# Token transposes moved up beside the inner layer's transposes in a mixture-of-experts loop

## The chip, the cores and the metric

The kernel runs on one core of one Trainium2 chip. The metric is the device time of one execution in microseconds (us), and less is better. TensorE is written PE, its weight loads PEld, VectorE DVE, ScalarE ACT, GpSimd POOL, SyncE SP.

## The reference

A decoder trunk of two layers over 512 tokens of width 1024, in float32. Layer 0 mixes tokens with an RWKV-7 recurrence, layer 1 with dilated window attention, and each layer ends with the mixture that this change is about:

```
h = h + hier_moe(rmsnorm(h, norm_ffn_g[layer]), ...)

# hier_moe: each token takes the best of 4 groups and in it 2 of 4 experts, so 2 of 16
for e in range(N_EXPERTS):                        # 16
    hdn = jax.nn.silu(t @ w_gate[e]) * (t @ w_up[e])   # t: 512 x 1024, hdn: 512 x 512
    y = y + gate[:, e:e + 1] * (hdn @ w_down[e])       # gate is 0 for tokens not routed to e
```

## The kernel before, in words

The function `moe` runs once for each layer. After a router it lists for each expert up to 128 tokens and takes the 16 experts one after another, in rounds: `rounds` unrolls round 0 and round 15 and runs rounds 1 to 14 in a loop of seven passes with two rounds each. All five engines run the same rounds, each with a program of its own, in its own written order; semaphores alone tie them together.

An expert's weights come in six pieces of 1 MB: two halves each of gate, up and down. SP loads a piece into one of six `raw` buffers (`load_piece`, L1442) as soon as DVE has freed one. Each piece is split into a high and a low part, so that a product in full precision is made of three faster ones: ACT writes `whi` (`split_hi`, L1448) and DVE writes `wlo` (`split_lo`, L1452, one piece a round in two halves, L1866). There are four buffers for each part. A `product` on PE is one piece: 12 matmuls of 128x512 (L1459, L1460, L1461).

Around the products, for one expert:

- POOL gathers the expert's token rows into `xg` with an indirect DMA (`fetch`, L1629 and L1632). There is one `xg`, so `fetch` waits until PE has transposed the expert before. Behind it on POOL stands `store_output` of an earlier expert (L1543, L1547), which waits for that expert's output `yo` from ACT, and then for its own DMA.
- `pe_tokens` (L1466 to L1472) transposes `xg` into PSUM banks 0 and 1: 16 transposes of 64x64. It waits for the gather and for DVE to be done with those banks. ACT and DVE then split the result into `xhi` (L1503) and `xlo` (L1508). Both exist twice, so x stands in four tiles, and the tokens of expert e+1 are made while those of e are read.
- `pe_gate` and `pe_up` are two products each, into banks 2 and 3. ACT makes `sg` (L1515), DVE makes `hid` (L1522).
- `pe_hidden` (L1475 to L1481) transposes `hid` into banks 4 and 7: 8 transposes of 64x64. ACT and DVE split it into `hhi` (L1527) and `hlo` (L1532).
- `pe_down` is two products, into banks 5 and 6, and ACT copies each to `yo` (L1540).

The down product of expert e-1 is done in round e. A round of PE before the change is, with numbers of pieces behind the names: gate(e) 0, hidden(e-1), gate(e) 1, down(e-1) 0, down(e-1) 1, tokens(e+1), up(e) 0, up(e) 1.

Of the kernel before, what the change touches and what calls it, by code (L numbers as in the profile page):

```python
# [1335 lines left out]
def moe(nc, io, g, layer, result=None):  # L1336
# [7 lines left out]
    with Scope(nc, f"moe{layer}") as s:  # L1344
# [54 lines left out]
        def loop_sems(tag):  # L1399
            r = {x: s.sem(tag + x) for x in ["hi_ok", "split_ok", "piece_used", "xt_done", "xh_ok", "xl_ok", "sg_ok", "hid_ok", "ht_done", "hh_ok", "hl_ok",  # L1400
                                             "y_ok", "col_ok", "oc_ok", "xg_in", "y_st", "y_free"]}
            r["lead"] = 2 if tag else SPLITS
            r["raw_in"] = [s.sem(f"{tag}raw_in{i}") for i in range(6)]
            return r

        main, more = loop_sems(""), loop_sems("more_")
# [14 lines left out]
        def token_list(out, rows):  # L1421

            for k in range(2):
                for j in range(J):
                    ins = nc.tensor.matmul(out, rows[:, k, j, :], mtok[:, k, j, :], start=k == 0 and j == 0, stop=k == 1 and j == J - 1)
            return ins
# [6 lines left out]
        def start(eng, m, names):  # L1433
            for x in names:
                eng.sem_inc(m[x], {"split_ok": 6, "piece_used": m["lead"]}.get(x, 1))
# [18 lines left out]
        def product(pe, m, n, slot, b, hi, lo, k0, begin, end):  # L1454

            pe.wait_ge(m["split_ok"], n + 7)
            wh, wl = (w[slot % SPLITS][:, :].rearrange("p (k n) -> p k n", k=4) for w in (whi, wlo))
            for k in range(4):
                nc.tensor.matmul(bank[b][:, :], hi[:, k0 + k, :], wh[:, k, :], start=begin and k == 0, stop=False)  # L1459
                nc.tensor.matmul(bank[b][:, :], hi[:, k0 + k, :], wl[:, k, :], start=False, stop=False)  # L1460
                ins = nc.tensor.matmul(bank[b][:, :], lo[:, k0 + k, :], wh[:, k, :], start=False, stop=end and k == 3)  # L1461
            ins.then_inc(m["piece_used"], 1)


        def pe_tokens(pe, m, c):
            pe.wait_ge(m["xg_in"], c * 16 + 16)  # L1466
            pe.wait_ge(m["xl_ok"], c * 2 + 1)
            pe.sem_inc(pe_turn, 1)
            for kt in range(KT):
                for b in range(2):  # L1470
                    ins = nc.tensor.transpose(bank[b][:, 64 * kt:64 * kt + 64], xg[side(b), P * kt:P * kt + P], g["ident"][side(b), side(b)])  # L1471
            ins.then_inc(m["xt_done"], 1)  # L1472

        def pe_hidden(pe, m, c):
            pe.wait_ge(m["hid_ok"], c + 2)  # L1475
            pe.wait_ge(m["hl_ok"], c * 2 + 1)
            pe.sem_inc(pe_turn, 1)
            for kt in range(FH // P):
                for b in range(2):
                    ins = nc.tensor.transpose(bank[4 + 3 * b][:, 64 * kt:64 * kt + 64], hid[side(b), P * kt:P * kt + P], g["ident"][side(b), side(b)])  # L1480
            ins.then_inc(m["ht_done"], 1)  # L1481

        def pe_gate(pe, m, c, x, half, n, slot):
            if half == 0:
                pe.wait_ge(m["xl_ok"], c * 2 + 3)
                pe.wait_ge(m["sg_ok"], c + 1)
            product(pe, m, n, slot, 2, xhi[x], xlo[x], 4 * half, half == 0, half == 1)
# [66 lines left out]
        def piece(e, x, k):  # L1554

            if isinstance(e, int) and e == 0:
                return k, k, 1
            return e * 6 + (k - 2), (6 * x + k - 2) % 12, e + (0 if k < 2 else 1)
# [387 lines left out]
        @block.tensor  # L1946
        def _(pe):
            start(pe, main, ["piece_used", "xt_done", "ht_done"])

            def keep_busy(times):  # L1950

                for _ in range(times):
                    nc.tensor.matmul(bank[3][:, 0:P], g["ident"][:, :], g["ident"][:, :], start=True, stop=True)  # L1953

            keep_busy(4)
            for j in range(J):
                pe.wait_ge(xn_ok, j + 1)
                for kt in range(KT):
                    ins = nc.tensor.transpose(bank[kt][:, P * j:P * j + P], xn[:, j, P * kt:P * kt + P], g["ident"][:, :])  # L1959
                    if j == J - 1:  # L1960
                        ins.then_inc(tr, 1)
            pe.wait_ge(par_in, PAR)
            for kt in range(KT):
                pe.wait_ge(ev_d if kt % 2 else ev_a, kt // 2 + 1)
                c = 32 * (kt % 4)
                last = nc.tensor.matmul(bank[0][c:c + 32, :], wr[:, kt, :], xnT[:, kt, :], start=kt < 4, stop=kt >= 4)  # L1966
            last.then_inc(lgT_done, 1)
            pe.wait_ge(lgT_ok, 1)
            for j in range(J):
                ins = nc.tensor.matmul(bank[1][:, (NG + NE) * j:(NG + NE) * (j + 1)], lgT[:, P * j:P * j + P], g["quarters"][:, :], start=True, stop=True)  # L1970
            ins.then_inc(lg_done, 1)
            keep_busy(12)
            pe.wait_ge(ms_ok, 1)
            nc.tensor.matmul(bank[7][:, P:P + NE], g["upper"][:, :], msum[:, :], start=True, stop=True)
            nc.tensor.matmul(bank[7][:, P + NE:P + 2 * NE], g["ones"], msum[:, :], start=True, stop=True).then_inc(rank_done, 1)
            keep_busy(8)
            pe.wait_ge(mtok_ok, 4)
            pe.wait_ge(hot_ok, 2)
            token_list(bank[7][:, 0:2 * NE], hot).then_inc(idx_mm, 1)
            keep_busy(16)  # L1980
            pe_tokens(pe, main, 0)

            def round_(e, x):

                first, last = (isinstance(e, int) and e == v for v in (0, NE - 1))
                k = iter(range(6))
                at = lambda: piece(e, x, next(k))[:2]
                pe_gate(pe, main, e, x, 0, *at())
                if not first:
                    pe_hidden(pe, main, e - 1)  # L1990
                pe_gate(pe, main, e, x, 1, *at())
                if not first:
                    for half in range(2):
                        pe_down(pe, main, e - 1, half, *at())
                if not last:
                    pe_tokens(pe, main, e + 1)
                else:
                    pe.wait_ge(pick_ok, 1)
                    pe.wait_ge(main["xl_ok"], 2 * NE + 1)
                    for j in range(J):  # L2000
                        ins = nc.tensor.transpose(bank[0][:, P * j:P * j + P], picks[:, j, :], g["ident"][:, :])
                    ins.then_inc(pick_done, 1)
                for half in range(2):
                    pe_up(pe, main, e, x, half, *at())

            rounds(pe, round_)
            pe_hidden(pe, main, NE - 1)
            for half in range(2):
                pe_down(pe, main, NE - 1, half, *piece(NE, 0, half)[:2])
            pe.wait_ge(main["y_ok"], 2 * NE + 1)  # L2010
            pe.wait_ge(pick_T, 1)
            for j in range(J):
                for half in range(2):
                    nc.tensor.matmul(last_bank(j, half)[:, :], picksT[:, j, :], yo[:, 512 * half:512 * half + 512], start=True, stop=True).then_inc(last_mm, 1)
            with overflow(pe):
                start(pe, more, ["piece_used", "xt_done", "ht_done"])
                for b in range(1, J):
                    pe.wait_ge(late_hot, 2 * b)
                    ins = token_list(bank[7][:, 2 * NE * b:2 * NE * b + 2 * NE], late[b])
                ins.then_inc(late_mm, 1)  # L2020
                pe.wait_ge(last_ok, 2 * J)

                def further_round(e, b, c):
                    pe_tokens(pe, more, c)
                    for k, part in enumerate([pe_gate, pe_up]):
                        for half in range(2):
                            part(pe, more, c, 0, half, c * 6 + (2 * k + half), 2 * k + half)
                    pe_hidden(pe, more, c)
                    for half in range(2):
                        pe_down(pe, more, c, half, c * 6 + (4 + half), 4 + half)  # L2030

                each_further(pe, further_round)
# [647 lines left out]
```

## Time and profile before

| | |
|---|---|
| three runs, median | 1526.06 us |
| three runs, lowest and highest | 1524.58 and 1527.32 us |
| the profiled execution, its own time | 1526.37 us |
| its span, first to last instruction | 1524.6 us |
| PE, DVE, ACT, POOL busy | 1364.3, 1020.4, 847.2, 382.7 us |
| mean granted TensorE clock | 0.95 |

The time of an execution is its span and 1.77 us around it. The two expert loops run from 546 to 836 us and from 1208 to 1498 us of the span, roughly. Matmuls overlap on PE, so each stands in the trace for longer than the distance to the next one: what one costs is the distance between two starts.

### The profile page before, as it was taken

To read this page: it belongs to the slowest core of one execution; us is meant where nothing else is said; L and a number is where in the kernel's file an instruction comes from. 1 tells how busy PE (TensorE), PEld (TensorE's weight loads), DVE (VectorE), ACT (ScalarE), POOL (GpSimd) and SP (SyncE) were. 2 spreads that over 40 slices of the span, in tenths; PEclk is the share of its full clock that TensorE was granted. 3 is DMA by queue.
4 is the path that set the end of the run, shared out by engine and by line. 5 is a ranking of instruction groups with operands and counts; after the bars stand their busy time and mean duration, and the time that the engine had idled before them with its cause. 6 is when DMAs were issued, how large, how long until landed. Compare 5 with 4: busy or idle time off the path is not lost. (4 is left out here: it accounts for less than half of the span.)

```text
span 1524.6 us, 29683 instructions
## 1 busy us (share of the span) xinstructions
PE 1364.3 (89%) x11603; PEld 1067.1 (70%) x11603; DVE 1020.4 (67%) x1354; ACT 847.2 (56%) x1266; POOL 382.7 (25%) x419
## 2 busy tenths in 40 slices
PE   5999896776779899999999699999989899999994
PEld 2476685666664578887887487778777678788782
DVE  6357642455634489889997734675444798999896
ACT  6635542444421258887886334444552488788882
POOL 1022244436550003332223200002120123222223
PEclk9999897999999889999999899999988899999997
DMA  5231300052442579999996432121101899999984
GB/s 174 84 110 56 138 0 16 16 157 88 134 155 104 196 266 377 383 377 379 378 385 229 163 99 83 56 84 56 56 29 49 300 351 383 381 380 375 380 318 172
DMA packets 172105, 301.88 MB, mean 198 GB/s; under 512 B 34637, under 2 KB 45005, under 8 KB 172000
## 3 DMA queue, kind: packets, MB, share of 16 engines
q1 hardware_dynamic: 159488, 271.53, 49.9%
q0 software_dynamic: 11232, 24.61, 4.5%
q10 hardware_dynamic: 1280, 4.26, 0.7%
q8 instruction: 76, 1.25, 0.3%
q14 instruction: 29, 0.24, 0.0%
HBM read 279.96 MB, written 34.60 MB: 206 GB/s over the span
## 5 line engine op out<-in xcount | busy, mean ns | idle before, releaser
L1452 DVE TENSOR_TENSOR moe_wlo<-moe_raw,moe_whi 128x2048 fp32r<-128x2048 f32 x162 | 370.0, 2287 | 37.4 <-ACT moe_whi L1448 33.1
L1448 ACT ACTIVATE moe_whi<-moe_raw 128x2048 fp32r<-128x2048 f32 x192 | 366.8, 1916 | 23.7 <-PE all_bank L1461 22.4
L1459 PE MATMUL all_bank<-moe_whi,moe_xhi 128*128 128x512 f32 x512 | 208.7, 408 | 4.1 <-DVE moe_xlo L1508 4.1
L1460 PE MATMUL all_bank<-moe_wlo,moe_xhi 128*128 128x512 f32 x512 | 200.9, 392 | 0.0
L1461 PE MATMUL all_bank<-moe_whi,moe_xlo 128*128 128x512 f32 x512 | 200.7, 392 | 0.0
L1459 PEld LDWEIGHTS all_bank<-moe_whi,moe_xhi 128*128 128x128 f32 x512 | 96.8, 189 | 27.6 <-DVE moe_xlo L1508 4.4
L1629 POOL COPY moe_idxcol<-moe_idx 128x1 int32 (+1 forms) x30 | 33.8, 1128 | 315.4 <-PE all_bank L1471 315.4
L1461 PEld LDWEIGHTS all_bank<-moe_whi,moe_xlo 128*128 128x128 f32 x512 | 96.8, 189 | 21.4
L1460 PEld LDWEIGHTS all_bank<-moe_wlo,moe_xhi 128*128 128x128 f32 x512 | 97.1, 190 | 18.2
L1459 PE MATMUL all_bank<-moe_whi,moe_hhi 128*128 128x512 f32 x256 | 100.0, 391 | 3.3 <-issue 2.6
L1461 PE MATMUL all_bank<-moe_whi,moe_hlo 128*128 128x512 f32 x256 | 99.6, 389 | 0.0
L1460 PE MATMUL all_bank<-moe_wlo,moe_hhi 128*128 128x512 f32 x256 | 99.6, 389 | 0.0
L2136 DVE SCALAR_TENSOR_TENSOR attn_wlo<-attn_xhat,all_par,attn_whi 128x512 fp32r<-128x512 f32 x64 | 43.8, 746 | 80.2 <-ACT attn_whi L2119 80.2
L907 ACT ACTIVATE chunks_pw<-all_bank 128x256 f32<-128x256 f32 x144 | 48.4, 387 | 60.6 <-PE all_bank L1248 41.7
L2458 PE MATMUL all_bank<-attn_xhi,attn_whi 128*128 128x512 f32 x192 | 77.9, 406 | 1.6 <-DVE attn_wlo L2130 1.0
L2460 PE MATMUL all_bank<-attn_xhi,attn_wlo 128*128 128x512 f32 x192 | 75.9, 396 | 0.0
L2459 PE MATMUL all_bank<-attn_xlo,attn_whi 128*128 128x512 f32 x192 | 75.8, 395 | 0.0
L1866 DVE TENSOR_TENSOR moe_wlo<-moe_raw,moe_whi 128x1024 fp32r<-128x1024 f32 x60 | 72.9, 1215 | 0.0
L1032 DVE TENSOR_TENSOR chunks_pw<-all_bank,chunks_pw 64x256 f32<-64x256 f32 x64 | 27.0, 422 | 67.6 <-PE all_bank L1256 66.3
L1543 POOL COPY moe_outcol<-moe_outidx 128x1 int32 (+1 forms) x30 | 54.3, 1809 | 23.1 <-DMA out_dram<-moe_yo,moe_outcol 23.1
L358 PE MATMUL all_bank<-project_xhi,project_whi 128*128 128x512 f32 x128 | 52.1, 407 | 7.7 <-DVE rwkv_rw_n L662 4.1
L1459 PEld LDWEIGHTS all_bank<-moe_whi,moe_hhi 128*128 128x128 f32 x256 | 48.0, 188 | 14.2 <-issue 4.3
(442 smaller groups left out, 2982.2 us busy)
## 6 DMA issues: line engine op xcount, KB each, us to landing
moe_raw<-in_moe_w_gate_dram SPq DMA_DIRECT2D x64, 1024.0 KB, 10.3
moe_raw<-in_moe_w_up_dram SPq DMA_DIRECT2D x64, 1024.0 KB, 9.6
moe_raw<-in_moe_w_down_dram SPq DMA_DIRECT2D x64, 1024.0 KB, 9.0
attn_xhat<-in_w_kv_dram SPq DMA_DIRECT2D x10, 1024.0 KB, 5.0
out_dram<-all_gain SPq DMA_DIRECT2D x16, 512.0 KB, 3.9
attn_xhat<-in_attn_w_q_dram SPq DMA_DIRECT2D x6, 1024.0 KB, 5.0
all_h<-in_rwkv_w_k_dram SPq DMA_DIRECT2D x4, 1024.0 KB, 9.2
all_h<-in_rwkv_w_v_dram SPq DMA_DIRECT2D x4, 1024.0 KB, 5.1
```

The lines of the kernel that those rows point to most:

```text
L358: mm(b[:, :], hi[0], hi[1], start=first, stop=False)
L907: inc(nc.scalar.activation(dst, src, ACT.Copy), name)
L1448: nc.scalar.activation(whi[slot % SPLITS][:, :], raw[slot % 6][:, :], ACT.Copy).then_inc(m["hi_ok"], 1)
L1452: nc.vector.tensor_tensor(wlo[slot % SPLITS][:, :], raw[slot % 6][:, :], whi[slot % SPLITS][:, :].bitcast(fp32), ALU.subtract).then_inc(m[ ...
L1459: nc.tensor.matmul(bank[b][:, :], hi[:, k0 + k, :], wh[:, k, :], start=begin and k == 0, stop=False)
L1460: nc.tensor.matmul(bank[b][:, :], hi[:, k0 + k, :], wl[:, k, :], start=False, stop=False)
L1461: ins = nc.tensor.matmul(bank[b][:, :], lo[:, k0 + k, :], wh[:, k, :], start=False, stop=end and k == 3)
L1543: nc.gpsimd.tensor_copy(outcol[:, :], outidx[:, bass.ds(col, 1)]).then_inc(m["oc_ok"], 1)
L1866: ins = nc.vector.tensor_tensor(wlo[slot % SPLITS][:, cols], raw[slot % 6][:, cols], whi[slot % SPLITS][:, cols].bitcast(fp32), ALU.subtract)
L2458: nc.tensor.matmul(out, a[0], b[0], start=begin, stop=False)
L2459: nc.tensor.matmul(out, a[0], b[1], start=False, stop=False)
L2460: return nc.tensor.matmul(out, a[1], b[0], start=False, stop=end)
```

## The change

In rounds 1 to 14 the transposes of the coming expert's tokens are issued directly behind those of the inner layer, between the two gate products, and no longer between the down and the up products. Round 0, which has no inner layer to transpose yet, keeps its place for them, and so does the last round with its own transposes of `picks`. The tiles, the waits of each step and the programs of all other engines are unchanged.

```diff
                 pe_gate(pe, main, e, x, 0, *at())
                 if not first:
                     pe_hidden(pe, main, e - 1)
+                    if not last:
+                        pe_tokens(pe, main, e + 1)
                 pe_gate(pe, main, e, x, 1, *at())
                 if not first:
                     for half in range(2):
                         pe_down(pe, main, e - 1, half, *at())
-                if not last:
+                if first:
                     pe_tokens(pe, main, e + 1)
-                else:
+                if last:
                     pe.wait_ge(pick_ok, 1)
                     pe.wait_ge(main["xl_ok"], 2 * NE + 1)
```

On PE, in the first round of the loop of layer 0, this is what stands around the inner layer's transposes before. `ISA` and `REGISTER_ALU` rows are the waits and the registers of a step.

```order
1221 L1461 MATMUL all_bank<-moe_whi,moe_xlo 128x512
1222 L1476 ISA
1223 L1480 MATMUL all_bank<-all_ident,moe_hid 128x64 x8
1224 L1456 REGISTER_ALU
1225 L1459 MATMUL all_bank<-moe_whi,moe_xhi 128x512
```

And in the changed kernel, at the same place:

```order
1221 L1461 MATMUL all_bank<-moe_whi,moe_xlo 128x512
1222 L1476 ISA
1223 L1480 MATMUL all_bank<-all_ident,moe_hid 128x64 x8
1224 L1466 ISA
1225 L1467 ISA
1226 L1471 MATMUL all_bank<-all_ident,moe_xg 128x64 x16
1227 L1456 REGISTER_ALU
1228 L1459 MATMUL all_bank<-moe_whi,moe_xhi 128x512
```

The 16 token transposes with their two waits now stand between the 8 of `hid` and the second gate product. The place that they left, on PE between the second down product and the first up product, was this before:

```order
1263 L1461 MATMUL all_bank<-moe_whi,moe_hlo 128x512
1264 L1466 ISA
1265 L1467 ISA
1266 L1471 MATMUL all_bank<-all_ident,moe_xg 128x64 x16
1267 L1456 REGISTER_ALU
1268 L1459 MATMUL all_bank<-moe_whi,moe_xhi 128x512
```

And is this now:

```order
1265 L1460 MATMUL all_bank<-moe_wlo,moe_hhi 128x512
1266 L1461 MATMUL all_bank<-moe_whi,moe_hlo 128x512
1267 L1456 REGISTER_ALU
1268 L1459 MATMUL all_bank<-moe_whi,moe_xhi 128x512
1269 L1460 MATMUL all_bank<-moe_wlo,moe_xhi 128x512
```

The up product follows the down product without transposes between them. No other engine's order changes.

## Rows read from the trace of the kernel before

**Rows 1.** The page: span, and busy time by engine

```profile
span 1524.6 us, 29683 instructions
PE 1364.3 (89%) x11603; PEld 1067.1 (70%) x11603; DVE 1020.4 (67%) x1354; ACT 847.2 (56%) x1266; POOL 382.7 (25%) x419
```

**Rows 2.** One round of each layer: length, busy time by engine, clock, DMA

```profile
core 0: us, PE busy (x) PEld busy (x) DVE busy (x) ACT busy (x) POOL busy (x), PEclk, DMA share, GB/s
616.54:634.37 17.83, 17.83 (x99) 14.26 (x98) 16.09 (x13) 14.60 (x13) 5.30 (x4) 1.00 1.03 386
1296.68:1314.51 17.83, 17.83 (x99) 14.27 (x98) 16.10 (x13) 14.61 (x13) 5.30 (x4) 1.00 1.04 377
```

**Rows 3.** Waits in ten rounds, 600 to 780 us: total, times, longest

```profile
DVE moe_hid L1522 <- PE all_bank L1461: 6.0, 10, 0.6
...
PEld all_bank L1480 <- issue: 3.5, 10, 0.4
```

**Rows 4.** PE in time around the inner layer's transposes: start, duration, what

```profile
633.37 0.39 PE L1461 MATMUL all_bank<-moe_whi,moe_xlo 128*128 128x512 f32 x1
...
634.05 0.39 PE L1461 MATMUL all_bank<-moe_whi,moe_xlo 128*128 128x512 f32 x1
634.37 0.46 PE L1480 MATMUL all_bank<-all_ident,moe_hid 64*128 64x64 f32 x8
634.76 0.50 PE L1459 MATMUL all_bank<-moe_whi,moe_xhi 128*128 128x512 f32 x1
635.09 0.40 PE L1460 MATMUL all_bank<-moe_wlo,moe_xhi 128*128 128x512 f32 x1
```

**Rows 5.** PE in time around the token transposes of the same round

```profile
625.02 0.39 PE L1461 MATMUL all_bank<-moe_whi,moe_hlo 128*128 128x512 f32 x1
625.34 0.71 PE L1471 MATMUL all_bank<-all_ident,moe_xg 64*128 64x64 f32 x16
625.98 0.50 PE L1459 MATMUL all_bank<-moe_whi,moe_xhi 128*128 128x512 f32 x1
626.32 0.40 PE L1460 MATMUL all_bank<-moe_wlo,moe_xhi 128*128 128x512 f32 x1
```

**Rows 6.** PE in time in round 1, at the first down product

```profile
566.18 0.49 PE L1459 MATMUL all_bank<-moe_whi,moe_hhi 128*128 128x512 f32 x1 [0.34 <-DVE moe_hlo L1532]
```

**Rows 7.** DVE makes `hid`; PE's sequencer at `pe_hidden` (ns min/median/max, when)

```profile
631.91 0.69 DVE L1522 TENSOR_TENSOR moe_hid<-all_bank,moe_sg 128x512 f32<-128x512 f32 x1 [0.60 <-PE all_bank L1461]
...
L1477 PEldq EVENT_SEMAPHORE  x1: 51/51/51, 632.7 to 632.7; - x1
```

**Rows 8.** POOL in time in one round; then landings of all L1632, and all L1547

```profile
626.22 1.27 POOL L1629 COPY moe_idxcol<-moe_idx 128x1 int32 x1 [10.72 <-PE all_bank L1471]
628.34 1.05 POOL L1632 DMA_INDIRECT moe_xg<-xn_dram,moe_idxcol  x1 [0.85 <-POOL moe_idxcol L1629]
...
DMA to landing us min/median/max: 4.3/6.6/7.2
...
DMA to landing us min/median/max: 3.7/6.9/7.7
```

**Rows 9.** DMA in two rounds, 40 slices; gate pieces' landing, 600 and 1290 us

```profile
GB/s 407 372 375 395 400 283 285 395 416 363 397 407 407 409 414 384 409 414 386 384 395 235 255 384 393 347 361 404 407 377 409 407 393 411 404 338 407 407 308 375
DMA packets 6852, 13.47 MB, mean 378 GB/s; under 512 B 521, under 2 KB 521, under 8 KB 6852
...
moe_raw<-in_moe_w_gate_dram SPq DMA_DIRECT2D x2, 1024.0 KB, 8.6
...
moe_raw<-in_moe_w_gate_dram SPq DMA_DIRECT2D x3, 1024.0 KB, 11.8
```

**Rows 10.** A late gate piece in layer 1: issue, landing, ACT's split of it

```profile
1307.79 0.37 SPq L1442 DMA_DIRECT2D moe_raw<-in_moe_w_gate_dram  x1
...
DMA to landing us min/median/max: 12.1/12.1/12.1
...
1321.18 1.91 ACT L1448 ACTIVATE moe_whi<-moe_raw 128x2048 fp32r<-128x2048 f32 x1
```

## The prediction, made before the changed kernel was run

> **What bounds the kernel now.** I read the page first: PE is busy 89% of a span of 1524.6 us, DVE 67% [rows 1]. That is a mean over stages, so I cut out single rounds of the expert loop, the only place the change touches. A round takes 17.83 us in either layer, and PE is busy 17.83 of them, at full clock; DVE has 16.1 us of work and ACT 14.6 [rows 2]. The list of waits over ten rounds agrees: DVE waits for PE, and PE for nobody; its weight loads alone stand idle, 0.35 us ahead of the inner layer's transposes [rows 3]. So in the steady rounds PE's own stream sets the time, and an edit gains what it takes out of that stream, as long as no other engine is longer than the new round.
>
> Busy is not the same as fast, though. PE's timeline shows matmuls 0.227 us apart: two steps of the list at 633.37 to 634.05 hold three of them, 0.68 us [rows 4]. 72 matmuls at 0.227 are 16.34 us, and the round is 17.83. The remaining 1.49 us are the transposes and the stumbling around them.
>
> **What a group of transposes costs.** From the last matmul ahead of the 8 transposes of `hid` (634.05) to the second behind them (635.09) is 1.04 us [rows 4]. Two ordinary distances would be 0.45, so this group costs 0.59. For the 16 token transposes the same reading is 625.02 to 626.32, 1.30 us, less 0.45, so 0.85 [rows 5]. Eight transposes more cost 0.26, which is 0.0325 each. So of the 0.59 only 8 x 0.0325 = 0.26 is transposing, and 0.33 is fixed. It can be seen where: the first transpose comes 0.32 us after the last matmul, where 0.227 is usual (0.09); the first matmul comes 0.39 us after the first transpose, and not 0.26 (0.13); the second matmul comes 0.33 us behind the first (0.11) [rows 4]. The token group shows the same 0.32, and 0.34 at its end [rows 5].
>
> **What the change removes.** Two groups of this kind become one. 24 transposes in one group cost 0.33 + 24 x 0.0325 = 1.11 us, against 0.59 + 0.85 = 1.44: 0.33 us less a round. The two groups explain 1.44 of the 1.49 us that a round has over its matmuls; the other 0.05 lies in a few distances of 0.24 just behind each group, and I count half of it as going too. That gives 0.35 us a round. It happens in 14 rounds of two layers: 28 x 0.35 = 9.8 us.
>
> What the border between the two groups costs instead is not in the trace, since the groups never touch. The lower bound is nothing: both are 64x64 transposes against the identity. The upper bound is that the step into a group (0.09) is paid again, or that the three small sequencer steps of `pe_tokens` stand open. The sequencer executed the like step of `pe_hidden` at 632.7, while its first transpose ran at 634.37 [rows 4, 7]; it is 1.6 us ahead, so its steps lie under the gate product. Were that cover gone, three steps like the one of 51 ns [rows 7] would be 0.15 us. I take zero, since the sequencer's lead is the nearer row, and keep 0.09 to 0.15 for the range, 2.5 to 4.2 us in all.
>
> The Trainium skill, in "TensorEngine Tiling (Array Packing)", section Key Properties, says that changing the tiling mode, and not just the tile, drains TensorE. Matmuls here are 128*128 and transposes 64*128 in the rows, so by that rule the fixed part is the price of two changes of mode, and the border between two groups of one mode is free; the sum by the rule is the same 9.8 us, and its other reading, a price of each group whatever stands beside it, would be 28 x 0.05 or less.
>
> **A wait that goes too.** In round 1 PE stands 0.34 us at the first down product for `hlo` [rows 6]. That product now comes some 0.5 us later behind the transposes of `hid` (24 instead of 8 transposes between them), so the wait is covered. Once a layer, 0.7 us in all. Together 10.5 us.
>
> **What is moved, and what it is moved past.** The transposes pass three products: gate 1, down 0 and down 1, about 8.2 us. Four things hang on them.
>
> The gather of the next tokens starts when the transposes are done. `fetch` begins 0.9 us after their start and issues its DMA 3.0 us after it, and it lands at most 7.2 us later [rows 5, 8]: 10.2 us after the transposes of one round, and the next come 17.5 us after them. Since use and refill move together, this slack is the same as before. Only the step from round 0, which keeps its place, into round 1 is shortened by the three products. There the next group comes some 9.5 us after the last (three products, both groups' own transposes), against 3.0 to the issue and 4.3 to 7.2 to the landing [rows 8]: 7.3 to 10.2. I take the least, since the queue is still short at the start of a loop, and so no wait; the other end would be 0.7 us once a layer, 1.4 in all.
>
> On POOL, `store_output` stands behind `fetch` and now has to wait for `yo`, which comes, as I estimate from 36 distances of 0.227, 0.65 us of transposes and about a us for the copy on ACT, 9.7 us after the start of the token transposes. It is issued a us later and lands after at most 7.7 [rows 8], at 18.4, and the next `fetch` would start at 18.4 too (17.5 + 0.9). If it should be late by a fraction, 7 us of slack of the gather cover it. SP's queue is not touched.
>
> ACT and DVE take the tokens where they took them before, behind the copies of `yo`, and find them ready. `gate 1` ends 0.5 us later against `hid`, so ACT's `sg` and its next two splits shift by that within the round. DVE had 0.60 us of wait before `hid`, at 631.91 [rows 3, 7], and the shorter round takes 0.35 and the shift some 0.5 of its free time. So DVE comes to `hid` about when PE allows it, perhaps 0.1 to 0.2 late. PE needs `hid` at 634.37 and has it at 632.60, 1.8 us ahead [rows 4, 7]. DVE's 16.1 us still fit into 17.48.
>
> The weights must come faster. Two rounds move 13.47 MB [rows 9]. In 16 of the 40 slices of that stretch they come at over 400 GB/s [rows 9]; at 400, 6.74 MB take 16.8 us, and the new round of 17.48 leaves 0.7. But there is a warning: gate pieces land 8.6 us after their issue early in layer 0, and 11.8 in layer 1 [rows 9]. The queue ahead of them is filling at today's pace. One of them lands at 1319.9, and ACT takes it at 1321.18: 1.3 us of slack [rows 10]. I come back to it as a rival.
>
> **The sum.** 9.8 + 0.7 = 10.5 us off the profiled execution's 1526.37 is 1515.9; the median of the runs is 0.3 below that execution, so I forecast 1515.6 us.
>
> **The rivals.**
>
> *The border costs its step.* The three sequencer steps or a second step into a group are paid. 2.5 to 4.2 us of the gain stay out: 1518.1 to 1519.8. For it: nothing in the trace shows two groups in a row. Against it: the sequencer's lead of 1.6 us.
>
> *DMA holds part of it.* If the 378 GB/s of two whole rounds [rows 9] is all that the DMA engines can do with gathers and stores among the loads, each round shortened by 0.35 us adds as much to the queue. That is hidden until the slack is used up: 1.3 us before ACT waits [rows 10], and 1.8 us more that `hid` has ahead of PE [rows 4, 7], so 3.1 us a layer of 4.9. The gain is then 6.2 + 0.7 = 6.9: 1519.2. For it: the landings that grow, and a DMA share over 1 in rows 2. Against it: slices of the same rounds over 400 GB/s.
>
> *No change.* The Trainium skill has a rule for this. "DMA: Bandwidth & Descriptors", section Where 436 GB/s comes from, says that for transfers between HBM and SBUF the HBM side, about 358 GB/s, binds. By it a round of 6.74 MB could not be under 18.8 us, and no order on PE would help. The trace disagrees, with 386 and 377 GB/s in rounds of 17.83 us [rows 2]. As a mechanism of this kernel: if loads were already what paces the round, taking stalls from PE gives 0, 1526.1. Against it stands that no row shows ACT waiting for a load.
>
> *Slower.* The gather becomes PE's wait. Token transposes in the middle of the gate product hold up everything behind them on PE: gate 1, both down products, and through them ACT's `sg` and the splits. It decides at a landing of 14.5 us (17.5 less the 3.0 to the issue), since the transposes then stand still for what is over. At 15 us it would be 0.5 us in each of 28 rounds, 14 us, against 9.8 gained: 1530. Gathers land after 7.2 us at most [rows 8]; but a weight piece took 12.1 [rows 10], so a queue of that length exists, and only its place on another queue keeps the gather out of it.
>
> **How the numbers follow.** Forecast 0.72, border 0.10, DMA in part 0.08, no change 0.06, slower 0.04. Runs of this kernel differ by 0.2%, 3 us, and that is about what a measurement can tell from no change. The first three are all faster by more than that: 0.90; same 0.06, slower 0.04. The range: the best case counts all of the 0.05 us and no cost, 28 x 0.38 + 0.7 = 11.3, or 1514.8, and a us for the spread of a median makes 1513.8. The other end takes in both rivals with a gain, 1519.8, so 1520.0. That leaves out the two last cases, 0.10, and some of the tails.
>
> **What would show it.** In the changed trace a steady round should be 17.48 us with PE busy throughout. There should be one group of 24 transposes of about 1.1 us from the matmul before it to the second behind it, over two ordinary distances; DVE's wait before `hid` near zero; POOL's wait for PE before `fetch` shorter, and a new wait for `yo` before the store; landings of gate pieces a us or so longer. A step would be wrong if the transposes of `xg` start later than 0.04 us after those of `hid` (the border), if ACT shows waits for loads late in layer 1 (DMA), or if PE waits for `xg`. The prediction fails as a whole if rounds are shorter but the time is not, or if PE gets waits in its place that the slack above should have covered.

## The result and the profile after

The changed kernel takes 1516.37 us (median of four runs, 1511.53 to 1516.56), and the kernel before beside it 1526.69 (four runs, 1524.58 to 1527.41). The ratio is 0.9927, 95% interval 0.9905 to 0.9949. The profiled execution took 1516.5 us with this page, which answers to [rows 1]:

```profile
span 1514.7 us, 29683 instructions
PE 1356.1 (90%) x11603; PEld 1066.0 (70%) x11603; DVE 1018.7 (67%) x1354; ACT 843.0 (56%) x1266; POOL 383.8 (25%) x419
...
PE 13%; DMA 5%; DVE 3%; ACT 1%; issue 1%; POOLq 0%; POOL 0%; DVEq 0%; SPq 0%; ACTq 0%
...
L1448 ACT ACTIVATE moe_whi<-moe_raw 128x2048 fp32r<-128x2048 f32 x192 | 365.2, 1918 | 37.5 <-DMA moe_raw<-in_moe_w_down_dram 14.6
```

The third row is the chain of work that ended last, and the last one the group of ACT's splits. In the kernel before that chain read so:

```profile
PE 19%; DVE 2%; issue 1%; DMA 1%; ACT 0%; POOLq 0%; POOL 0%; DVEq 0%; ACTq 0%
```

PE's share fell from 19% to 13%, and that of DMA rose from 1% to 5%. ACT now waits for weights, which it did nowhere in the ten rounds looked at before. So the gain came, and with it the first sign that something else has moved up to the edge.

The stretches that answer to [rows 2], with the same columns, are a steady round, round 1 of layer 0, all rounds 1 to 14 of layer 0, the last round of its loop, and then a late round, the fourteen rounds and the last round of layer 1:

```profile
629.42:646.86 17.44, 17.44 (x98) 14.27 (x98) 16.02 (x13) 14.37 (x13) 5.08 (x4) 1.00 1.03 386
...
559.52:577.10 17.58, 17.58 (x98) 14.19 (x97) 17.29 (x13) 14.39 (x13) 4.20 (x4) 1.00 1.00 363
559.52:804.38 244.86, 244.62 (x1346) 199.43 (x1346) 225.25 (x169) 201.52 (x182) 69.72 (x54) 1.00 1.03 384
804.38:821.00 16.62, 15.04 (x74) 11.86 (x74) 12.18 (x10) 10.62 (x11) 3.62 (x3) 1.00 0.41 159
1446.36:1464.38 18.02, 17.74 (x97) 14.17 (x96) 16.56 (x13) 15.95 (x14) 2.03 (x2) 1.00 1.05 396
...
1219.14:1464.38 245.24, 244.94 (x1345) 199.30 (x1344) 225.70 (x169) 202.06 (x182) 71.36 (x54) 1.00 1.03 384
1464.38:1480.96 16.58, 14.98 (x73) 11.85 (x73) 12.14 (x10) 10.56 (x11) 3.75 (x3) 1.00 0.46 172
```

A steady round lost 0.39 us. But the late one is 18.02, longer than any steady round before, and the last round of a loop is 16.62 and 16.58. In the kernel before round 1, the fourteen rounds of layer 0 and the last one were these:

```profile
562.41:812.63 250.22, 249.88 (x1345) 199.57 (x1345) 226.67 (x169) 204.41 (x182) 71.23 (x55) 1.00 1.02 379
812.63:828.50 15.87, 15.00 (x73) 11.84 (x73) 11.36 (x10) 10.27 (x10) 2.81 (x3) 1.00 0.27 104
562.41:580.88 18.47, 18.13 (x97) 14.18 (x96) 17.40 (x13) 14.60 (x13) 5.27 (x4) 1.00 0.99 356
...
1224.73:1490.78 266.05, 264.84 (x1417) 211.42 (x1417) 238.00 (x178) 214.70 (x192) 74.27 (x57) 1.00 0.98 365
```

The last of these lines is the whole loop of layer 1 with its last round. The loop of layer 0 went from 266.09 to 261.48 us, 4.6 less, and that of layer 1 from 266.05 to 261.82, 4.2 less. That is 8.8 of the 9.9 us between the spans. The other 1.1 us lie outside the loops, where the programs are the same: the first loop begins 2.9 us earlier (559.52, not 562.41), and the stretch between the loops is 1.9 us longer (398.1 us, not 396.2). In two more traces with one group, taken below, the first loop begins at 562.37 and 559.81 us. The programs of these stretches are the same in all of them, so I take the 1.1 us for chance and for no part of the gain.

PE's timeline around the one group that is left answers to [rows 4, 5]:

```profile
646.54 0.39 PE L1461 MATMUL all_bank<-moe_whi,moe_xlo 128*128 128x512 f32 x1
646.86 0.46 PE L1480 MATMUL all_bank<-all_ident,moe_hid 64*128 64x64 f32 x8
647.15 0.66 PE L1471 MATMUL all_bank<-all_ident,moe_xg 64*128 64x64 f32 x16
647.74 0.50 PE L1459 MATMUL all_bank<-moe_whi,moe_xhi 128*128 128x512 f32 x1
648.08 0.39 PE L1460 MATMUL all_bank<-moe_wlo,moe_xhi 128*128 128x512 f32 x1
```

From 646.54 to 648.08 it is 1.54 us; less two ordinary distances (0.45) that is 1.09, where 1.11 was forecast. The border lies between 646.86 and 647.15: 0.29, of which eight transposes are 0.26. It costs 0.03.

The list of waits over the same 180 us as in [rows 3]:

```profile
POOL moe_idxcol L1629 <- PE all_bank L1471: 57.3, 9, 6.5
POOL out_dram L1547 <- ACT moe_yo L1540: 50.7, 10, 5.2
...
ACT moe_whi L1448 <- DMA moe_raw<-in_moe_w_down_dram: 4.5, 6, 1.2
```

The wait of `hid` for PE (6.0 us before) is not in the list any more, POOL divides its idle time between PE and `yo`, and PE waits for no gather. New are ACT's waits for loads. In layer 0 the first is at 714 us, in a loop that begins at 559.52, and the weights land later there. Between 1400 and 1450 us of the changed kernel, from the issue of a weight piece to its landing it took:

```profile
DMA to landing us min/median/max: 12.6/13.4/13.5
```

In the kernel before, at the same rounds (1410 to 1460 us):

```profile
DMA to landing us min/median/max: 9.2/10.6/12.4
```

What that does at the end of a loop is seen in ACT's timeline of the last two rounds of layer 1, and in PE's:

```profile
1466.52 1.92 ACT L1448 ACTIVATE moe_whi<-moe_raw 128x2048 fp32r<-128x2048 f32 x1 [0.98 <-DMA moe_raw<-in_moe_w_up_dram]
```

```profile
1450.55 0.49 PE L1459 MATMUL all_bank<-moe_whi,moe_hhi 128*128 128x512 f32 x1 [0.28 <-DVE moe_hlo L1532]
...
1473.98 0.65 PE L2003 MATMUL all_bank<-all_ident,moe_xg 128*128 128x128 f32 x4 [0.73 <-DVE moe_xg L1881]
```

A piece lands late, ACT splits it late, DVE makes its low part late, and what stands behind that on DVE, `hlo` in one round and the rows for the `picks` in the last, is late for PE. PE never waits for a weight by name. In the last round its 0.73 us are nearly all of what that round gained in length (16.58 and 16.62 us, against 15.87).

### The profile page after: what moved, and what is told of

Same layout as the page of the kernel before. It is cut to its first block and busy times, and to the rows that moved or that the text cites. A ratio compares the mean times of both kernels' runs of the same rounds, so it can differ in the third digit from the quotient of the medians.

```text
span 1514.7 us, 29683 instructions
## 1 busy us (share of the span) xinstructions
PE 1356.1 (90%) x11603; PEld 1066.0 (70%) x11603; DVE 1018.7 (67%) x1354; ACT 843.0 (56%) x1266; POOL 383.8 (25%) x419
## 5 line engine op out<-in xcount | busy, mean ns | idle before, releaser
L1459 PE MATMUL all_bank<-moe_whi,moe_xhi 128*128 128x512 f32 x512 | 204.5, 399 | 4.4 <-DVE moe_xlo L1508 4.4
L1547 POOL DMA_INDIRECT out_dram<-moe_yo,moe_outcol x30 | 47.0, 1567 | 166.0 <-ACT moe_yo L1540 166.0
L1629 POOL COPY moe_idxcol<-moe_idx 128x1 int32 (+1 forms) x30 | 13.7, 457 | 192.9 <-PE all_bank L1471 159.3
## 6 DMA issues: line engine op xcount, KB each, us to landing
moe_raw<-in_moe_w_gate_dram SPq DMA_DIRECT2D x64, 1024.0 KB, 11.9
```

The costliest lines, as they stand in the source:

```text
L1547: pool.indirect_dma_start(out_dram, bass.IndirectOffsetOnAxis(ap=outcol[:, :], axis=0), yo[:, :], None, bounds_check=NE * T - 1, oob_is_er ...
```

## The experiments

Two questions were open. Is it the number of groups that pays, or their place? And does the DMA queue take part of the gain, as the rise of the landings suggests? The first three kernels ask the first. Each ratio below is to the kernel before, timed beside it on the same chip.

**The two kinds of transposes in the other order.** One group still.

```diff
                 if not first:
-                    pe_hidden(pe, main, e - 1)
                     if not last:
                         pe_tokens(pe, main, e + 1)
+                    pe_hidden(pe, main, e - 1)
```

> The changed kernel, with the token transposes ahead of those of the inner layer and not behind them; still one group of 24. If the gain is that of one group in place of two, it stays whole: rounds of 17.44 us as in the changed kernel, and 0.992 to 0.994 of before. If what helped was that the tokens stand behind the inner layer's (so that nothing delays hid), the inner layer's split comes 0.5 us later, down 0 waits for hlo, whose slack was 0.8 us, and part of the gain goes: 0.995 or more.

Measured: 1515.31 us, ratio 0.9926 (0.9900 to 0.9952). Steady rounds take 17.44 us, as in the changed kernel. The order inside the group doesn't matter.

**Moved, but apart.** The token transposes stand between gate 1 and down 0, so there are two groups as before, with `hlo` covered as in the changed kernel.

```diff
                     pe_hidden(pe, main, e - 1)
-                    if not last:
-                        pe_tokens(pe, main, e + 1)
                 pe_gate(pe, main, e, x, 1, *at())
+                if not first and not last:
+                    pe_tokens(pe, main, e + 1)
```

> The token transposes are moved up by two products, between gate 1 and down 0, so that they are earlier but touch no other group. If the gain is that of one group in place of two, there is none here: rounds of 17.83 us and 1.000 of before, within 0.001. If the gain came of tokens that are ready earlier (ACT that does not wait, a gather that starts earlier), most of it is here too: 0.994 to 0.996.

Measured: 1524.56 us, ratio 0.9994 (0.9980 to 1.0008), no difference that can be measured. Round 1 and a steady round in its trace:

```profile
561.73:579.56 17.83, 17.83 (x97) 14.27 (x97) 17.30 (x13) 14.38 (x13) 5.50 (x4) 1.00 1.00 357
633.04:650.87 17.83, 17.83 (x98) 14.27 (x98) 16.02 (x13) 14.36 (x13) 5.64 (x4) 1.00 1.01 381
```

The steady round is the old one. Only round 1 is shorter, 17.83 instead of 18.47, so the place is worth that wait and nothing else. All the rest of the gain is the joining.

One thing more can be read from this kernel. Its rounds are as long as those of the kernel before, and from the issue of a weight piece to its landing it took, between 600 and 618 us and then between 744 and 762:

```profile
DMA to landing us min/median/max: 7.7/8.3/9.5
...
DMA to landing us min/median/max: 8.1/8.8/10.0
```

In the kernel before the medians of the same two windows are 7.8 and 9.8 us, and in the changed kernel 9.3 and 13.2. So at rounds of 17.83 us the queue of loads can keep up, or very nearly, and at 17.44 it falls behind.

**Three groups.** The kernel before with its 16 token transposes in two groups of eight, a down product between them.

```diff
-                    for half in range(2):
-                        pe_down(pe, main, e - 1, half, *at())
-                if not last:
+                    pe_down(pe, main, e - 1, 0, *at())
+                    if not last:
+                        pe_tokens(pe, main, e + 1, range(0, 4))
+                    pe_down(pe, main, e - 1, 1, *at())
+                if first:
                     pe_tokens(pe, main, e + 1)
+                elif not last:
+                    pe_tokens(pe, main, e + 1, range(4, 8))
```

The range is a new argument of `pe_tokens`; that part of the edit is not shown.

> The kernel before, with the token transposes cut into two groups of 8, one between the two down products and one where all were. The same 24 transposes in a round, in three groups. By the fixed price of a group of 0.33 to 0.38 us, which PE pays as it is what bounds a round, rounds get 18.2 us and the whole 9.2 to 10.6 us longer: 1.006 to 1.007 of before. If the queue of loads bounds at 17.8 us just as PE does, this is unchanged, as PE is then over it. If the price is only that of a change of the matrix that is read, or hidden: 1.000.

Measured: 1538.17 us, ratio 1.0090 (1.0068 to 1.0113). The first of the two half groups on PE's timeline, with the matmuls beside it:

```profile
640.80 0.39 PE L1461 MATMUL all_bank<-moe_whi,moe_hlo 128*128 128x512 f32 x1
641.12 0.46 PE L1472 MATMUL all_bank<-all_ident,moe_xg 64*128 64x64 f32 x8
641.52 0.50 PE L1459 MATMUL all_bank<-moe_whi,moe_hhi 128*128 128x512 f32 x1
641.85 0.40 PE L1460 MATMUL all_bank<-moe_wlo,moe_hhi 128*128 128x512 f32 x1
```

It has the 0.32 us ahead, the 0.40 to the first matmul and the 0.33 to the second that [rows 4] showed for `hid`. A steady round is 18.24 us, 0.41 over the old one, and 28 x 0.41 = 11.5 is just the distance of the spans, 1536.1 and 1524.6. The medians lie 13.1 us apart, and the interval of the ratio, 10.4 to 17.2 us, holds the 11.5. The ratio is above the 1.006 to 1.007 that was expected, in part since the fixed price had been put at 0.33 to 0.38. So a group more costs 0.41 and a group less gives 0.39: the price of a group is measured from both sides.

**A shorter PE stream still.** The changed kernel without the matmuls that multiply the low part of x in the up product: eight fewer in a round, 1.8 us of PE. The output changes by what that leaves out. If PE paced the rounds, they would shorten by it.

```diff
+                if b == 3:
+                    ins = nc.tensor.matmul(bank[b][:, :], hi[:, k0 + k, :], wl[:, k, :], start=False, stop=end and k == 3)
+                    continue
                 nc.tensor.matmul(bank[b][:, :], hi[:, k0 + k, :], wl[:, k, :], start=False, stop=False)
```

> The changed kernel, without the third matmul pass of the up products (lo times high part), so that PE has 8 matmuls or 1.8 us less in every round; the output misses that term. If PE alone bounds the changed kernel's rounds, they fall until DVE's 16.1 us bind: 16.1 to 16.5, and the whole is 26 to 36 us under the changed kernel, 0.970 to 0.976 of before. If the load queue can't do a round in less than some 17.8 us, as the growing landings say, only the slack of the six buffers is left to gain: the whole is 2 to 6 us under the changed kernel, 0.988 to 0.992 of before, and ACT waits for loads in most rounds.

Measured: 1518.87 us, ratio 0.9959 (0.9943 to 0.9975). That is not faster than the changed kernel, and 0.004 above the 0.988 to 0.992 that was expected if the loads hold it: in the time nothing shows of the 1.8 us a round. Its second round and eight rounds further on:

```profile
578.04:594.28 16.24, 16.14 (x88) 12.72 (x89) 15.82 (x13) 14.16 (x14) 4.48 (x4) 1.00 1.05 398
645.84:789.31 143.47, 131.07 (x704) 101.78 (x705) 129.54 (x97) 115.77 (x104) 53.89 (x32) 1.00 1.03 381
```

Three rounds are short, and two pass over to what follows. Then eight take 143.47 us, 17.93 each, with PE idle for 12.4 of them. The waits, and DMA, between 600 and 780 us:

```profile
ACT moe_whi L1448 <- DMA moe_raw<-in_moe_w_down_dram: 16.4, 19, 1.3
```

```profile
DMA packets 34902, 68.69 MB, mean 382 GB/s; under 512 B 2608, under 2 KB 2608, under 8 KB 34902
...
moe_raw<-in_moe_w_gate_dram SPq DMA_DIRECT2D x20, 1024.0 KB, 13.4
```

The loads pace this kernel: a piece lands after 13.4 us, and over 180 us 382 GB/s is what comes, though the short round at 578 us had 398. Six pieces in 17.93 us, each 13.4 us on its way, are 4.5 buffers in flight on average (an estimate from these two numbers); the others are being split. The queue's own round is thus some 17.9 us long here. That is clearly above the 17.44 of the changed kernel, which runs ahead of its loads and lives on the lead with which a loop begins. Whether it is above the 17.83 of the kernel before is not shown: the landings of that kernel grew slowly, and those of the kernel with the moved but separate groups, at the same 17.83, stood still.

**The same loads, lighter.** To see what that costs, three kernels load only half the rows of each down piece, so 1 MB of the 6.8 of a round less. The other half of the buffer keeps what stood in it, and the output changes. The edit is the same in the kernel before, the changed kernel, and the one with the shorter PE stream.

```diff
+            if kind == "down":
+                sp.dma_start(raw[slot % 6][:, 0:1024].rearrange("p (k n) -> p k n", k=2),
+                             w[:, 0:256, :].rearrange("a (k p) n -> p (a k) n", p=P)).then_inc(m["raw_in"][slot % 6], 16)
+                return
```

In the kernel before:

> The kernel before, in which the loads of the down pieces bring only the first half of their rows (1 MB less of 6.8 MB in a round; the rest of the buffer is stale, so the output is not the reference's). It is the base for the next one. If PE alone bounds the rounds of before, nothing changes: rounds of 17.83 us, 1.000 of before, within 0.002. If loads held it anywhere, it is faster.

Measured: 1525.0 us, ratio 0.9994 (0.9974 to 1.0015). All rounds 2 to 14 stay at 17.83. The kernel before was not held by its loads.

In the changed kernel:

> The changed kernel with the same lightened loads. If the load queue took part of the gain, at the end of each loop (rounds of 17.75 to 18.03 us and a longer last one), it gives it back here: all 28 rounds at 17.44, 11.5 to 12 us off the lightened kernel before and 2.5 to 3 us more than the change gained with full loads: 0.991 to 0.9925 of before. If the loads took nothing and the late rounds have another cause, they stay as they are, and it is 0.993 to 0.994.

Measured: 1515.56 us, ratio 0.9934 (0.9910 to 0.9957). Its interval overlaps with the changed kernel's, so the total doesn't tell whether the loads cost it 3 us. The trace of the loop does, by rounds 1 to 14 and the last round of layer 0:

```profile
564.86:809.20 244.34, 244.34 (x1346) 199.51 (x1346) 225.42 (x169) 201.17 (x182) 77.06 (x54) 1.00 0.95 329
809.20:825.04 15.84, 14.97 (x73) 11.85 (x73) 11.37 (x10) 10.28 (x10) 3.49 (x3) 1.00 0.10 38
```

260.18 us, against 261.48 with full loads and 266.09 before. With light loads the loop gives 5.9 us, 11.8 in two layers. The loads take back 1.3 us of it in layer 0 and, by the same subtraction from 261.82, 1.6 in layer 1.

With the shorter PE stream:

> The changed kernel with 8 matmuls less in a round and with the lightened loads. With full loads the 1.8 us that PE saved came to nothing, and rounds stood at 17.9 us after the first three. If that was the load queue, whose floor falls with its bytes to about 15.2 us, rounds are now 16.1 to 16.4 us throughout, as DVE's work is 16.1: 0.966 to 0.972 of before. If it was the waits between ACT, DVE and PE, rounds stay near 17.9 and it is 0.993 or more.

Measured: 1482.46 us, ratio 0.9722 (0.9685 to 0.9759). Now the stretch that held at 17.93 a round is short throughout, the fourteen rounds of layer 0 taking 16.25 each:

```profile
558.93:786.41 227.48, 225.76 (x1233) 178.10 (x1233) 222.64 (x169) 199.07 (x182) 59.74 (x54) 1.00 0.98 350
```

The same 1.8 us of PE work that gave nothing with full loads gives 1.2 us a round when there are fewer bytes to load (17.45 on average with light loads, now 16.25). The 16.24 us of the early rounds with full loads are the same. The other 0.6 us do not come; DVE is busy 15.9 of the 16.25 us, so it is the next engine to look at, but that it holds these rounds was not tested. What stops the next gain in the changed kernel is thus settled: it is the loads.

**Longer runs for the loads.** If the queue is the limit, its rate is worth a try. Gate and up pieces come as 2 KB runs per partition; here each partition reads one run of 8 KB, and the k order of x follows by reading the token transposes with a stride of four columns. The result is the same.

```diff
-                    ins = nc.tensor.transpose(bank[b][:, 64 * kt:64 * kt + 64], xg[side(b), P * kt:P * kt + P], g["ident"][side(b), side(b)])
+                    ins = nc.tensor.transpose(bank[b][:, 64 * kt:64 * kt + 64], xg[side(b), 512 * (kt // 4):512 * (kt // 4) + 512].rearrange("t (p k) -> t p k", k=4)[:, :, kt % 4], g["ident"][side(b), side(b)])
...
+            if kind != "down":
+                sp.dma_start(raw[slot % 6][:, :], w.rearrange("a (p k) n -> p (a k n)", p=P)).then_inc(m["raw_in"][slot % 6], 16)
+                return
```

With the shorter PE stream, where loads are the bound:

> The kernel with 8 matmuls less in a round and full loads, in which each partition takes four neighbouring rows of a gate or up piece, 8 KB in one run, and not four rows of 2 KB that lie 256 KB apart (the token transposes pick every fourth column to match). The same bytes. Rounds of the load queue were 17.9 us with 2 KB runs. If short runs are what keeps it below the 400 GB/s of its best slices, the floor falls, to 17.0 to 17.5, and the whole is 0.980 to 0.990 of before. If the runs don't matter, since what costs is the gathers and stores between the loads, the rounds stay at 17.9 and the whole at 0.996.

Measured: 1507.76 us, ratio 0.9893 (0.9851 to 0.9935), against 0.9959 without the long runs. Four late rounds, and DMA between 600 and 780 us:

```profile
659.72:729.62 69.90, 66.69 (x355) 52.29 (x354) 64.73 (x49) 57.39 (x52) 28.71 (x16) 1.00 1.01 391
```

```profile
DMA packets 20284, 70.99 MB, mean 394 GB/s; under 512 B 2709, under 2 KB 2709, under 8 KB 15027
```

The queue's own round falls from 17.93 to 69.90 / 4 = 17.48 us, about as 394 GB/s against 382 would have it (17.4); in the late rounds alone it is 391 against 381.

In the changed kernel, and in the kernel before:

> The changed kernel with full loads, and with gate and up pieces in runs of 8 KB. The load queue's floor was 17.44 us a round with such runs, as long as PE's new round. If the queue is what the changed kernel still waits for late in each loop, those waits are gone: all rounds at 17.44, 2.5 to 3 us off the changed kernel, 0.991 to 0.992 of before. If it makes up only a part, some late rounds stay over 17.5.

> The kernel before with runs of 8 KB. PE bounds its rounds at 17.83 and its loads kept up by means of their slack, so nothing changes: 1.000 of before, within 0.002; landings late in each loop are 2 us or more shorter than 11.8. If strided token transposes cost PE anything, it shows here as longer rounds.

Measured: 1530.08 us, ratio 1.0036 (1.0019 to 1.0052), and 1542.97 us, ratio 1.0109 (1.0082 to 1.0135). Both are slower. The rounds became 17.92 and 18.28 us, 0.48 and 0.45 more, and between 600 and 780 us of the first one ACT has no more waits for loads. PE's timeline of the first of the two shows where the time is:

```profile
637.29 1.12 PE L1474 MATMUL all_bank<-all_ident,moe_xg 64*128 64x64 f32 x16
638.34 0.50 PE L1462 MATMUL all_bank<-moe_whi,moe_xhi 128*128 128x512 f32 x1
```

The 16 token transposes take 1.05 us to the next matmul and not 0.59. A transpose that reads every fourth column costs 0.029 us more than 0.0325, nearly twice as much. The loads were helped, and PE, which paces the rounds, paid. The kernel before lost 4.6 us more than 28 x 0.45 = 12.6 by its span (1541.8 us). The trace has this part outside the loops, 3.9 us of it between them (835.67 to 1235.75 us, against 828.50 to 1224.73 before); its cause was not looked for.

**The changed kernel again**, on the chip of those two, since medians of single chips had differed:

> The changed kernel once more, as the partner of the first on the same chip: 0.993 of before, late rounds of 17.7 to 18.0 us.

Measured: 1518.09 us (12 runs, 1513.69 to 1522.22), ratio 0.9956 (0.9940 to 0.9972), so 6.7 us faster and not 10.3. Steady rounds are 17.44 here too. Late ones in layer 0 are 18.38 and 17.97. The two loops take 262.42 and 261.34 us, 8.4 less than before, where the first trace of this kernel had 8.8 less. So the late rounds are not what divides the two comparisons, and their intervals overlap. The gain of this change is then 7 to 10 us, with 8.4 and 8.8 in the loops of the two traces.

**Long runs without the strided read.** The last kernel puts the order of columns where x is written once a layer, on DVE, so that gathers and token transposes stay contiguous; the router's weights are loaded in the same order. Only the edit on DVE is shown.

```diff
-                nc.vector.scalar_tensor_tensor(out=xn[:, j, :], in0=h[:, j, :], scalar=rstd[:, j:j + 1], in1=gb[:, :], op0=ALU.mult, op1=ALU.mult).then_inc(xn_ok, 1)
+                for b in range(2):
+                    cols = slice(512 * b, 512 * b + 512)
+                    ins = nc.vector.scalar_tensor_tensor(out=xn[:, j, cols].rearrange("p (k q) -> p q k", k=4), in0=h[:, j, cols].rearrange("p (q k) -> p q k", k=4),
+                                                         scalar=rstd[:, j:j + 1], in1=gb[:, cols].rearrange("p (q k) -> p q k", k=4), op0=ALU.mult, op1=ALU.mult)
+                ins.then_inc(xn_ok, 1)
```

> Runs of 8 KB for gate and up as before, but the token transposes read neighbouring columns again: the order of the columns is changed once a layer, where DVE writes the normalised tokens (eight writes of 512 columns, every fourth one apart by 128), and the router's weights are loaded in the same order. If strided reading was the whole price of the first such kernel, rounds are 17.44 us and stay so to the end of each loop; the loops are 2.5 to 3 us shorter than the changed kernel's. DVE's strided writes are the open cost: 0 to 1.2 us a tile of tokens, at most 9.6 in all, if it too halves its rate. 0.991 to 0.992 of before if they are free, 0.997 if they cost all that.

Measured: 1516.76 us, ratio 0.9946 (0.9928 to 0.9965). Rounds 1 to 14 of layer 0, its last round, and the landing of gate pieces between 600 and 780 us:

```profile
566.04:810.34 244.30, 244.30 (x1345) 199.50 (x1344) 225.45 (x169) 201.17 (x182) 85.06 (x54) 1.00 1.01 388
810.34:826.19 15.85, 14.98 (x74) 11.86 (x73) 11.38 (x10) 10.27 (x10) 2.50 (x3) 1.00 0.28 106
```

```profile
moe_raw<-in_moe_w_gate_dram SPq DMA_DIRECT2D x20, 1024.0 KB, 8.3
```

All bytes are loaded, and the loop is as short as with light loads, 260.15 us. Landings no longer grow. The 1.3 us of layer 0 thus come back with a faster queue just as with fewer bytes. But the writes of `moe_xn` on DVE, here and then in the changed kernel, are these:

```profile
515.97 7.64 DVE L1757 SCALAR_TENSOR_TENSOR moe_xn<-all_h,moe_rstd,all_gain 128x512 f32<-128x512 f32 x8
```

```profile
512.20 4.87 DVE L1752 SCALAR_TENSOR_TENSOR moe_xn<-all_h,moe_rstd,all_gain 128x1024 f32<-128x1024 f32 x4
```

The eight writes take 7.64 us from start to end, the four 4.87. They stand ahead of the router, where PE waits for them. From the first write to DVE's first copy of what PE then makes of them it is 2.4 us longer in layer 0 and 1.9 in layer 1, 4.3 in all, and the loops gain 3.0. None of the versions that do all the work is faster than the changed kernel.

## Why the prediction was right, and where it was not

The forecast of 1515.6 us is 0.8 us from the median, and the mechanism, one fixed price less in each round, is the one that the runs show. That the sum came so close is partly luck, as said below. Point by point:

- *A group of transposes has a fixed price of 0.33 us, and joining two saves 0.35 a round.* Right in kind and slightly low: 0.39 saved, 0.41 for a group more. The joined group is 1.09 us where 1.11 was forecast, and the small distances behind a group, of which the sum took half, went almost wholly: 17.44 less the 16.34 of 72 matmuls leaves 1.10. In 28 rounds that is 10.9 us and not 9.8.
- *The border costs nothing.* 0.03 us. The rival that the border costs a step (0.09 to 0.15) is out. The Trainium skill's rule in "TensorEngine Tiling (Array Packing)", section Key Properties, is that a change of tiling mode drains TensorE and a change of tile does not. The border inside one mode, 0.03, agrees with it. That the change of mode is what a group pays for is not shown; the rows are below.
- *The wait for `hlo` in round 1 gives 0.34 once a layer.* It is gone, but gave more. The step that moves it without joining took round 1 from 18.47 to 17.83, so 0.64. Of the changed kernel's 0.89 in round 1, 0.50 are over a steady round's gain. A pause costs more than its idle time; the last section has the rows.
- *`hid`, POOL and the gather have slack.* Right. DVE's wait before `hid` is gone and PE doesn't wait for it. POOL waits for `yo` as forecast, and PE never waits for the gather, so the slower rival did not come. Nor did loads pace the old rounds: the kernel before gains nothing from lighter loads.
- *The weights come in time.* This step failed. The text had it that at 400 GB/s, which 16 of 40 slices passed, 6.74 MB take 16.8 us. Slices over the mean say nothing of what the queue keeps up: where the loads set the pace it held 382 GB/s over 180 us, and a round of it is 17.9 us, longer than the changed kernel's 17.44. The warning in the text, 8.6 us to land and then 11.8, compared two loops; along the loops of the kernel before the growth is small (medians of all pieces of 7.8 us at 600 and 9.8 at 744, 9.7 at 1264 and 10.1 at 1408), and it is the changed kernel whose landings run up to 13.2 and 13.4 us. The rival that DMA holds part of the gain had a chance of 0.08 and came true in part. Its price was put at 3.6 us of gain lost, and the traces of the two loops show 1.3 and 1.6. It came by the way that it named, ACT's slack used up first.

So the mechanism was right, and that the size came so near is luck in two ways. Two errors met: 1.1 us more from the joining and 0.3 from round 1, against some 3 us back to the loads. By the loops the terms are 28 x 0.39 + 2 x 0.50 = 11.9 less 2.9, 9.0, and the trace has 8.8, where 10.5 was forecast. The rest of the way to the measured 10.3 us lies outside the loops, where nothing was changed, and in the spread of the medians: the second comparison has 6.7.

Two things stay open. One is what in a group of transposes costs the 0.39 to 0.41 us. In the last round of the kernel before, four transposes of `picks` have the same 128*128 as the matmuls around them, so no mode changes there, and yet PE stumbles behind them:

```profile
821.48 0.66 PE L2001 MATMUL all_bank<-all_ident,moe_xg 128*128 128x128 f32 x4
821.90 0.48 PE L1459 MATMUL all_bank<-moe_whi,moe_xhi 128*128 128x512 f32 x1
822.21 0.40 PE L1460 MATMUL all_bank<-moe_wlo,moe_xhi 128*128 128x512 f32 x1
```

The second matmul behind them comes after 0.31 us, where 0.227 is usual and 0.33 stands behind `hid`. At least this part of the price is paid without a change of mode.

The other open thing is how much the loads cost in an execution that was not profiled. In three profiles with one group the two loops take 523.3, 523.8 and, with the kinds in the other order, 521.9 us, against 520.3 with light loads, so the loads cost 3, 3.4 and 1.6 us there. It varies from execution to execution, and by less than the 3.6 us between the two comparisons of the changed kernel.

## What to carry to other kernels

Where PE paces a loop, count the groups of small transposes among its full matmuls, not the transposes: one group fewer gave 0.39 us, 16 transposes themselves cost 0.52. Before spending a PE gain, look whether the landings of the weight loads grow along the loop. In the changed kernel they grew from 9.3 to 13.2 us in 144 us of the first loop, and ACT waited for no weight until 714 us, well inside it. A loop outruns its queue on the slack of its buffers while its list of waits shows nothing of it yet; a kernel with less PE work shows in one run how long the queue's own round is.

## What the hardware showed that was not expected

- Weight loads with gathers and stores beside them held 382 GB/s with 2 KB runs and 394 with 8 KB runs for two pieces in three. The Trainium skill, "DMA: Bandwidth & Descriptors", section Where 436 GB/s comes from, has some 358 GB/s as the binding rate on the HBM side; no run here was bound that low. The Trainium skill, "Perfetto Trace Analysis", section Engine Utilization, has that a single active core can pull more than that share, and the 382 and 394 GB/s agree.
- A transpose of 64x64 in float32 costs 0.0325 us, and 0.061 when it reads every fourth column.
- DVE took 7.64 us for eight writes of 512 columns in a strided order, and 4.87 for four of 1024 without, the same elements.
- A pause of PE ahead of a matmul cost more than the idle time that the profile gives it. At the first down product of the kernel before it is 0.34:

```profile
565.45 0.39 PE L1461 MATMUL all_bank<-moe_whi,moe_xlo 128*128 128x512 f32 x1
566.18 0.49 PE L1459 MATMUL all_bank<-moe_whi,moe_hhi 128*128 128x512 f32 x1 [0.34 <-DVE moe_hlo L1532]
566.51 0.39 PE L1460 MATMUL all_bank<-moe_wlo,moe_hhi 128*128 128x512 f32 x1
```

The start is 0.73 us after the last, where 0.227 is usual, and the next 0.33. That is 0.61 us lost for 0.34 of idle time, and nearly the 0.64 by which round 1 was longer than the others. The late round of the changed kernel is alike: 0.28 us of idle time, and 18.02 us is 0.58 longer than 17.44. Ahead of the transposes of `picks` it was not so: there 0.73 us of idle time made the last round 0.71 to 0.75 us longer.
